# Third weight tile behind a norm, feed-forward banks and the place of two ScalarE steps in a two-tower transformer kernel

## The chip, the cores and the metric
The kernel runs on one core of one Trainium2 chip. The metric is the device time of one execution in microseconds (us).

## The reference, cut to what matters
Two transformer blocks of model width 1024 follow each other on 512 latent tokens; 256 context tokens stand beside them. The first block has two layers, the second one layer with attention and one with a gating unit.

```python
for l in range(2):                                   # first block
    zx = modulate(rms_norm(x, norm1_g[l]), mx[0], mx[1]) @ w_in[l]      # and zc from ctx
    y_f = fourier_mix(zf, w_f)                       # DFT over positions and channels
    u = conv31(a * sigmoid(g)) + b_dw                # depthwise, 31 taps
    y_c = silu(layer_norm(u, ln_g, ln_b)) @ w_pw2    # the convolution's norm
    attn = latent attention, 8 heads of 64 + 32
    x = x + mx[2] * (concat([y_f, attn, y_c]) @ w_o[l])
    x = x + mx[5] * (square(relu(modulate(rms_norm(x)) @ w_mlp1)) @ w_mlp2)   # hidden 4096
x = rms_norm(x, final_norm_g)
for l in range(2):                                   # second block
    h = modulate(rms_norm(x), sh1, sc1)
    y = attention_mixer(h, ctx) if l == 0 else sgu_mixer(h)
    x = x + g1 * y
    z = conv3(modulate(rms_norm(x), sh2, sc2) @ w_up) + conv_b     # 2 * 2816 channels
    x = x + g2 * ((silu(z_gate) * z_up) @ w_down)
return rms_norm(x, final_norm)
```

`mx`, `sh`, `sc` and `g` are vectors made from the Silu of the conditions `c` by large weights (the modulation).

## The kernel before, in words
Activations lie transposed in SBUF: 128 channels on the partitions, tokens along the free dimension, eight chunks `k` of 128 channels. `CTX` is the 256 context tokens, `LAT` the 512 latent ones, `ALL` both.

Every product with a large weight is made in three terms, to get near fp32 from the faster fp32r format: each value is split in a high part and a low part, and a tile sums high x high, low activations x high weights, and high activations x low weights. The weights come as 346 tiles of 128 x 1024 through `w_raw` (four buffers). For tile `n` ScalarE copies the high part into `w_hi` (`split`, L758), and GpSimd subtracts for the low part into `w_lo` (`w_low`, L672). Both have two buffers, so tile `n` may be split only when TensorE is done with tile `n - 2`. `ahead(n)` on ScalarE is `split(n + 2)`; it stands at the head of tile `n`'s work there. TensorE waits for `lo_ready` before a tile, then runs 8 chunks x 3 terms = 24 matmuls for each of the column ranges.

Behind a norm the first two tiles are run together and in two column parts (`parted_pair`, L1524; `first_tokens`, L1559, for the token-major tiles of the gating unit), as the normed chunks come in one by one. The third tile behind a norm is then an ordinary one: L1406 (`tile`) in the input projections, L1812 (`quarter`) in the first block's feed-forward, L2004 (`turn` in `ffn`) in the second block's, L1424 (`token_major`) in the gating unit. It needs the first tile's weight buffer back, and the first tile's PSUM bank.

A tile's result goes to `bank(2 * (t % 2) + b)`; `b` is 0 for context and 1 for latent columns. Latent tiles thus alternate between banks 1 and 3. `drained[t % 2]` counts the tiles read out of them. In the second block's feed-forward (`ffn`) a turn of the loop has four tiles (gate, up, gate, up): ScalarE applies the middle tap (L1317), VectorE the two outer taps out of PSUM (L2753, L2758), ScalarE the Silu (L1324), VectorE the product (L2765), ScalarE its high part (L1328), VectorE its low part (L2768). In the first feed-forward of the second block, VectorE also makes modulation products (L2270) between them; in the first block's it makes them beside L2571, which empties the hidden tiles' banks.

The order on each engine is written out by hand. On ScalarE in the input projections of a layer: split, (second layer only: Silu of the conditions, L914), copy of the first tile out of PSUM (L879), next split, (first layer only: that Silu), square.

The latent attention loops over units of 256 queries (`d`). In iteration `d` TensorE runs scores of unit `d + 1` (L1671), pv of unit `d - 1` (L1732), the transposes of unit `d` (`turn`, L1718), and then the sums of the convolution's norm (`pe_ln`, L1747 and L1753) in a few late iterations. ScalarE runs `ev(d - 1)` (the copies of the transposed probabilities, L999, for which pv waits), projections' copies, `exps(d + 1)` (L988), `pv_hi(d - 1)` (L1010), and last `act_ln`, the norm's squares (L1018) or its root (L768, L770). The squares wait for VectorE (L2455), which waits for TensorE's first sum. VectorE's low part of pv's result is L2445; pv waits for it too.

Of the kernel before, what the change touches and what calls it, by code (L numbers as in the profile page):

```python
# [17 lines left out]

# [94 lines left out]
def two_towers(nc, a):  # L113
    ctx = ExitStack()
    with ctx:
# [633 lines left out]
        def _(act):  # L749
# [146 lines left out]
            for layer in (0, 1):  # L896
# [154 lines left out]
                for d in range(n_units + 1):  # L1051
                    if d:
                        ev(d - 1)
                    if d - 1 in behind:
                        proj_ev(behind[d - 1])
# [8 lines left out]
                    for x in ln_stages(layer, d):  # L1064
                        act_ln(*x)
# [234 lines left out]
            def ffn(layer, tb, shifts):  # L1300
                nf = N_FFN[layer]
                pair0 = 0
                for part, kk in enumerate(FFN_PARTS):
# [4 lines left out]
                    with act.Fori(0, kk // 2) as i:  # L1308
                        for j in range(4):
# [7 lines left out]
                            nc.scalar.activation(dst, bank(2 * (t % 2) + 1), ACT.Identity,  # L1317
# [77 lines left out]
        def _(pe):  # L1395
            def tile(n, j, t, cols, rhs_hi, rhs_lo, per_k=None, first=True):

                pe.wait_ge(lo_ready, n + 1)
                if first:
                    slot_free(t)  # L1400
                for k in range(8):
                    if per_k:
                        per_k(k)
                    for wt, x in ((whi3, rhs_hi), (whi3, rhs_lo), (wlo3, rhs_hi)):
                        for (s0, s1), b in both(cols):
                            mm = pe.matmul(bank(2 * (t % 2) + b, c1=s1 - s0), wt[:, j % 2, k, :],  # L1406
                                           x(k, s0, s1), start=(k == 0 and wt is whi3 and x is rhs_hi),
                                           stop=(k == 7 and wt is wlo3))
                mm.then_inc(tile_done, 1)

            def token_major(n, toks, b0, off, ready=None):

                for h in range(2):
                    pe.wait_ge(lo_ready, n + h + 1)
                    w_hi, w_lo = (x[:, (n + h) % 2].rearrange("p k m -> p (k m)")
                                  .rearrange("p (k m) -> p k m", k=4) for x in (whi3, wlo3))
                    for k in range(4):
                        kk = 4 * h + k
                        if ready:
                            ready(kk)  # L1420
                        for tok in range(toks):
                            xs = slice(off + tok * P, off + (tok + 1) * P)
                            for q, (x, wt) in enumerate(((hi3, w_hi), (lo3, w_hi), (hi3, w_lo))):
                                mm = pe.matmul(bank(b0 + tok // 2, c0=256 * (tok % 2),  # L1424
# [1654 lines left out]
```

## Time and profile before

| what | value |
|---|---|
| median of 3 runs | 2860.78 us (2856.76 to 2861.16) |
| the profiled execution's own time | 2860.61 us |
| its span in the profile | 2858.8 us |
| mean granted clock of TensorE | 0.995 |
| TensorE busy | 2755.0 us (96%) |
| ScalarE, VectorE, GpSimd busy | 1121.6, 1624.5, 1142.0 us |
| transfers | 303.89 MB, 106 GB/s on average |

The profile's rows are of one execution. PE is TensorE (PEld its weight loads), DVE VectorE, ACT ScalarE, POOL GpSimd; L1406 is line 1406 of the kernel. Times of rows are microseconds from the span's start. A busy TensorE is one with a matmul in flight; the clock that was granted to it is given as a share of 2.4 GHz.

### The profile page before, as it was taken

To read this page: it belongs to the slowest core of one execution; us is meant where nothing else is said; L and a number is where in the kernel's file an instruction comes from. 1 tells how busy PE (TensorE), PEld (TensorE's weight loads), DVE (VectorE), ACT (ScalarE), POOL (GpSimd) and SP (SyncE) were. 2 spreads that over 40 slices of the span, in tenths; PEclk is the share of its full clock that TensorE was granted. 3 is DMA by queue.
4 is the path that set the end of the run, shared out by engine and by line. 5 is a ranking of instruction groups with operands and counts; after the bars stand their busy time and mean duration, and the time that the engine had idled before them with its cause. 6 is when DMAs were issued, how large, how long until landed. Compare 5 with 4: busy or idle time off the path is not lost.

```text
span 2858.8 us, 39710 instructions
## 1 busy us (share of the span) xinstructions
PE 2755.0 (96%) x14728; PEld 2224.8 (78%) x14728; DVE 1624.5 (57%) x2354; ACT 1121.6 (39%) x1850; POOL 1142.0 (40%) x554
## 2 busy tenths in 40 slices
PE   6999899999999999999999999889999999999998
PEld 4755588888888766688888788668888889888887
DVE  4877576555646577478455654766634642533133
ACT  4345533121212436542233523664433444443242
POOL 1399333323232368144444331004444443444443
PEclk9999999999999999999999999999999999999999
DMA  7500043332333320035454211003544532222222
GB/s 288 211 1 1 1 148 112 110 129 107 123 112 118 114 108 1 23 114 200 165 191 155 74 67 38 1 9 104 185 161 141 189 118 89 79 98 96 96 96 81
DMA packets 83498, 303.89 MB, mean 106 GB/s; under 512 B 9120, under 2 KB 12704, under 8 KB 82464
## 3 DMA queue, kind: packets, MB, share of 16 engines
q1 hardware_dynamic: 83072, 298.43, 29.4%
q10 hardware_dynamic: 288, 3.55, 0.3%
q8 instruction: 96, 1.57, 0.2%
q14 instruction: 42, 0.34, 0.0%
HBM read 299.84 MB, written 2.10 MB: 106 GB/s over the span
## 4 chain that ended last, share of the span: by engine, by line
PE 56%; DVE 4%; ACT 2%; issue 2%; POOL 0%; DVEq 0%; ACTq 0%; POOLq 0%
PE psum L2004 16%; PE psum L1812 11%; PE psum L1406 9%; PE psum L2025 8%; PE psum L1424 2%; PE psum L1495 2%; PE psum L1879 1%; PE psum L1671 1%; DVE psum L2165 1%; PE psum L1900 1%; DVE tiny L2674 1%; DVE in_lo L2155 1%; PE psum L1690 0%; PE psum L1917 0%; PE psum L1732 0%
## 5 line engine op out<-in xcount | busy, mean ns | idle before, releaser
L672 POOL TENSOR_TENSOR w_lo<-w_raw,w_hi 128x1024 fp32r<-128x1024 f32 x346 | 865.3, 2501 | 1633.0 <-ACT w_hi L758 1632.9
L758 ACT ACTIVATE w_hi<-w_raw 128x1024 fp32r<-128x1024 f32 x346 | 366.9, 1060 | 1244.7 <-PE psum L1812 556.1
L2251 DVE SCALAR_TENSOR_TENSOR residual<-psum,modulation,residual 128x512 f32<-128x512 f32 (+1 forms) x150 | 99.6, 684 | 342.6 <-PE psum L1812 145.9
L2270 DVE CUSTOM_DVE_ANT_0 mod_w<-mod_w,conditions 128x1024 f32<-128x1024 f32 x176 | 288.4, 1648 | 3.3
L2004 PE MATMUL psum<-in_hi,w_hi 128*128 128x512 f32 x672 | 262.3, 390 | 3.8 <-POOL w_lo L672 3.8
L2004 PE MATMUL psum<-in_lo,w_hi 128*128 128x512 f32 x672 | 262.1, 390 | 0.0
L2004 PE MATMUL psum<-in_hi,w_lo 128*128 128x512 f32 x672 | 262.0, 390 | 0.0
L1812 PE MATMUL psum<-in_hi,w_hi 128*128 128x256 f32 (+1 forms) x720 | 218.6, 358 | 2.2 <-POOL w_lo L672 2.2
L1812 PE MATMUL psum<-in_hi,w_lo 128*128 128x256 f32 (+1 forms) x720 | 219.0, 359 | 0.0
L1812 PE MATMUL psum<-hidden_hi,w_hi 128*128 128x256 f32 (+1 forms) x720 | 218.3, 358 | 0.5 <-DVE hidden_lo L2537 0.2
L1812 PE MATMUL psum<-hidden_hi,w_lo 128*128 128x256 f32 (+1 forms) x720 | 218.4, 358 | 0.0
L1812 PE MATMUL psum<-in_lo,w_hi 128*128 128x256 f32 (+1 forms) x720 | 215.9, 355 | 0.0
L1812 PE MATMUL psum<-hidden_lo,w_hi 128*128 128x256 f32 (+1 forms) x720 | 215.5, 354 | 0.0
L1406 PE MATMUL psum<-in_hi,w_hi 128*128 128x256 f32 (+1 forms) x576 | 191.6, 376 | 3.3 <-ACT mixer_space L879 1.9
L1406 PE MATMUL psum<-in_hi,w_lo 128*128 128x256 f32 (+1 forms) x576 | 184.4, 363 | 0.0
L1406 PE MATMUL psum<-in_lo,w_hi 128*128 128x256 f32 (+1 forms) x576 | 183.3, 361 | 0.0
L2753 DVE SCALAR_TENSOR_TENSOR small_w<-psum,vectors,small_w 128x511 f32<-128x511 f32 x88 | 65.9, 749 | 186.3 <-ACT small_w L1317 186.2
L2571 DVE TENSOR_TENSOR scratch<-psum,scratch 128x256 f32<-128x256 f32 (+1 forms) x96 | 54.8, 598 | 187.5 <-ACT scratch L1097 187.5
L1812 PEld LDWEIGHTS psum<-in_hi,w_hi 128*128 128x128 f32 x720 | 135.8, 189 | 24.5 <-POOL w_lo L672 2.8
L1812 PEld LDWEIGHTS psum<-hidden_hi,w_hi 128*128 128x128 f32 x720 | 135.5, 188 | 24.1 <-DVE hidden_lo L2537 2.5
L1812 PEld LDWEIGHTS psum<-in_lo,w_hi 128*128 128x128 f32 x720 | 136.1, 189 | 20.8
L1812 PEld LDWEIGHTS psum<-hidden_lo,w_hi 128*128 128x128 f32 x720 | 135.7, 189 | 20.4
(322 smaller groups left out, 5935.8 us busy)
## 6 DMA issues: line engine op xcount, KB each, us to landing
w_raw<-stream_dram SPq DMA_DIRECT2D x346, 512.0 KB, 4.1
mod_w<-mods_dram SPq DMA_DIRECT2D x176, 512.0 KB, 3.5
mixer_space<-first_mods_dram SPq DMA_DIRECT2D x12, 512.0 KB, 14.8
small_w<-small_w_dram SPq DMA_DIRECT2D x2, 2048.0 KB, 13.5
in_hi_space<-dft_x_dram SPq DMA_DIRECT2D x2, 2048.0 KB, 8.9
residual<-tokens_dram ACTq DMA_DIRECT2D x1, 3072.0 KB, 10.6
in_lo_space<-first_mods_dram SPq DMA_DIRECT2D x4, 512.0 KB, 16.2
conditions<-conditions_dram SPq DMA_DIRECT2D x2, 1024.0 KB, 11.7
```

The lines of the kernel that those rows point to most:

```text
L672: nc.gpsimd.tensor_tensor(wlo[:, (j % 2) * 1024:(j % 2 + 1) * 1024], raw3[:, j, :], whi[:, (j % 2) * 1024:(j % 2 + 1) * 1024].bitcast(F32) ...
L758: nc.scalar.activation(whi[:, (j % 2) * 1024:(j % 2 + 1) * 1024], raw3[:, j, :], ACT.Copy).then_inc(hi_ready, 1)
L1406: mm = pe.matmul(bank(2 * (t % 2) + b, c1=s1 - s0), wt[:, j % 2, k, :], x(k, s0, s1), start=(k == 0 and wt is whi3 and x is rhs_hi), stop= ...
L1424: mm = pe.matmul(bank(b0 + tok // 2, c0=256 * (tok % 2), c1=256 * (tok % 2) + 256), x[:, kk, xs], wt[:, k, :], start=(kk == 0 and q == 0 a ...
L1495: mm = pe.matmul(part_out(t + i, cols, p), wt, x, start=(k, q) == terms[0], stop=(k, q) == terms[-1])
L1812: mm = pe.matmul(bank(2 * (t % 2) + b, c1=s1 - s0), wt[:, n % 2, k, :], x[:, k, s0:s1], start=(k == 0 and q == 0), stop=(k == 7 and q == 2))
L2004: mm = pe.matmul(bank(2 * (t % 2) + 1), wt[:, n % 2, k, :], x[:, k, NC_:T], start=(k == 0 and q == 0), stop=(k == 7 and q == 2))
L2025: mm = pe.matmul(bank(2 * (t % 2) + 1), wt[:, n % 2, block_no % 8, :], x[:, k, :], start=(k == 0 and q == 0), stop=(k == kk - 1 and q == 2))
L2251: last = nc.vector.scalar_tensor_tensor(res3[:, m, s0:s1], bank(2 * (t % 2) + b, c1=s1 - s0), M(block_, chunk, m, 1 - b), res3[:, m, s0:s1 ...
L2270: nc.vector.tensor_tensor_reduce(w_tile, w_tile, cvec[:, 0:D], 1.0, 0.0, ALU.mult, ALU.add, dots[:, q:q + 1]).then_inc(mod_done, 1)
L2571: last = nc.vector.tensor_tensor(x, bank(2 * (t % 2) + b, c1=s1 - s0), x, ALU.mult)
L2753: side = nc.vector.scalar_tensor_tensor(x[:, 1:NX], bank(2 * (t % 2) + 1, c1=NX - 1), vec[:, bass.ds(i * 4 + col, 1)], x[:, 1:NX], ALU.mul ...
```

## The change
It has four parts.
1. The third tile behind a norm (`third`) waits only for its high part, runs its 16 matmuls with high weights first, then waits for the low part and runs the other 8. It applies in both input projections, the first quarter of both feed-forwards of the first block, the first turn of both feed-forwards of the second, and the first half of the gating unit's second token-major pair.
2. The four tiles of a turn in `ffn` go to four banks (1, 3, 0, 2; `turn_out`). The third and fourth tiles of a turn wait for one drained tile less.
3. In the second layer of the first block the Silu of the conditions stands behind the next split, as in the first layer.
4. On ScalarE `act_ln` moves from the end of iteration `d` to behind `ev(d)` in the next iteration.

```diff
+        def turn_out(t, j):
+            return bank(2 * ((t + j) % 2) + 1 - j // 2)
...
-                if layer:
-                    condition_silu()
                 copy_out(t0, lambda x, y: ckv[:, 0, x:y], ALL)
                 at_step(1)
-                if not layer:
-                    condition_silu()
+                condition_silu()
...
                 for d in range(n_units + 1):
                     if d:
                         ev(d - 1)
+                        for x in ln_stages(layer, d - 1):
+                            act_ln(*x)
...
                         pv_hi(d - 1)
-                    for x in ln_stages(layer, d):
-                        act_ln(*x)
...
-            def tile(n, j, t, cols, rhs_hi, rhs_lo, per_k=None, first=True):
-                pe.wait_ge(lo_ready, n + 1)
+            def tile(n, j, t, cols, rhs_hi, rhs_lo, per_k=None, first=True, third=False):
+                pe.wait_ge(hi_ready if third else lo_ready, n + 1)
                 if first:
                     slot_free(t)
-                for k in range(8):
-                    if per_k:
+                for k, q in terms(third):
+                    if per_k and q == 0:
                         per_k(k)
...
+                    if third and (k, q) == (0, 2):
+                        pe.wait_ge(lo_ready, n + 1)
...
+            def terms(third):
+                return sorted([(k, q) for k in range(8) for q in range(3)],
+                              key=lambda x: third and x[1] == 2)
...
-                    tile(n0 + j, (n0 + j) % 4, t0 + j, cols, in_hi, in_lo)
+                    tile(n0 + j, (n0 + j) % 4, t0 + j, cols, in_hi, in_lo, third=j == 2)
...
+                            third = first and j == 2
-                            pe.wait_ge(lo_ready, i * 4 + (n + 1))
-                            pe.wait_ge(drained[t % 2], i * 2 + t // 2)
+                            pe.wait_ge(hi_ready if third else lo_ready, i * 4 + (n + 1))
+                            pe.wait_ge(drained[t % 2], i * 2 + t // 2 - j // 2)
...
-                                    mm = pe.matmul(bank(2 * (t % 2) + 1), wt[:, n % 2, k, :],
+                                mm = pe.matmul(turn_out(tb_part, j), wt[:, n % 2, k, :],
...
-                token_major(N_SGU + 2 * c, 4, 2 * (t % 2), NC_)
+                token_major(N_SGU + 2 * c, 4, 2 * (t % 2), NC_, third=c == 1)
```

`quarter` and `token_major` are changed as `tile` is; ScalarE and VectorE read the turns' banks by `turn_out` too.

## Rows read from the trace of the kernel before

**Rows 1.** The page's busy times, with shares of the span and instructions.
```profile
PE 2755.0 (96%) x14728; PEld 2224.8 (78%) x14728; DVE 1624.5 (57%) x2354; ACT 1121.6 (39%) x1850; POOL 1142.0 (40%) x554
```
**Rows 2.** TensorE's waits: line, who ended them, total us, times, longest us.
```profile
PE psum L2004 <- POOL w_lo L672: 3.8, 2, 1.9
...
PE psum L1732 <- ACT in_hi_space L999: 3.5, 2, 2.8
...
PE psum L1812 <- POOL w_lo L672: 2.2, 2, 1.9
...
PE psum L1406 <- POOL w_lo L672: 0.6, 2, 0.4
```
**Rows 3.** Timeline of TensorE: start, duration, instruction, in brackets the idle time before.
```profile
989.39 0.47 PE L1406 MATMUL psum<-in_hi,w_hi 128*128 128x512 f32 x1 [1.89 <-ACT mixer_space L879]
...
1254.22 0.50 PE L1812 MATMUL psum<-in_hi,w_hi 128*128 128x512 f32 x1 [1.87 <-POOL w_lo L672]
...
1981.22 0.47 PE L2004 MATMUL psum<-in_hi,w_hi 128*128 128x512 f32 x1 [1.93 <-POOL w_lo L672]
...
2349.45 0.35 PE L1424 MATMUL psum<-w_hi,in_hi 128*128 128x256 f32 x1 [1.26 <-POOL w_lo L672]
...
2496.53 0.64 PE L1524 MATMUL psum<-in_hi,w_lo 128*128 128x256 f32 x4
...
2499.08 0.47 PE L2004 MATMUL psum<-in_hi,w_hi 128*128 128x512 f32 x1 [1.92 <-POOL w_lo L672]
```
**Rows 4.** Windows: us, TensorE busy (matmuls), granted clock, DMA share, GB/s.
```profile
316.00:320.00 4.00, 4.00 (x33) 0.57 0.02 4
336.00:341.00 5.00, 4.55 (x38) 0.66 0.00 0
1254.00:1259.00 5.00, 4.78 (x14) 0.66 0.00 0
...
2499.00:2504.00 5.00, 4.92 (x22) 1.00 0.60 202
```
**Rows 5.** Timeline of ScalarE, second layer's input projections.
```profile
984.20 1.06 ACT L758 ACTIVATE w_hi<-w_raw 128x1024 fp32r<-128x1024 f32 x1 [3.64 <-PE psum L1524]
...
986.57 1.91 ACT L914 ACTIVATE conditions<-conditions 128x2048 f32<-128x2048 f32 x1
```
**Rows 6.** Timelines of VectorE and ScalarE, second layer's first feed-forward tiles.
```profile
1252.26 0.69 DVE L2571 TENSOR_TENSOR scratch<-psum,scratch 128x512 f32<-128x512 f32 x1 [3.05 <-ACT scratch L1097]
...
1258.49 0.68 DVE L2571 TENSOR_TENSOR scratch<-psum,scratch 128x512 f32<-128x512 f32 x1
...
1261.63 1.06 ACT L758 ACTIVATE w_hi<-w_raw 128x1024 fp32r<-128x1024 f32 x1 [1.79 <-PE psum L1812]
```
**Rows 7.** Timelines of VectorE, ScalarE and GpSimd, second block's first feed-forward turn.
```profile
1982.13 3.38 DVE L2270 CUSTOM_DVE_ANT_0 mod_w<-mod_w,conditions 128x1024 f32<-128x1024 f32 x1
...
1988.59 1.06 ACT L758 ACTIVATE w_hi<-w_raw 128x1024 fp32r<-128x1024 f32 x1
...
1989.73 2.40 POOL L672 TENSOR_TENSOR w_lo<-w_raw,w_hi 128x1024 fp32r<-128x1024 f32 x1 [5.30 <-ACT w_hi L758]
...
1992.02 1.22 DVE L2270 CUSTOM_DVE_ANT_0 mod_w<-mod_w,conditions 128x1024 f32<-128x1024 f32 x1
...
1994.03 1.06 ACT L758 ACTIVATE w_hi<-w_raw 128x1024 fp32r<-128x1024 f32 x1 [3.72 <-PE psum L2004]
```
**Rows 8.** Timelines of VectorE, TensorE and ScalarE around the first layer's convolution norm.
```profile
313.94 0.58 DVE L2445 TENSOR_TENSOR in_lo<-psum,in_hi 64x128 fp32r<-64x128 f32 x2
...
315.98 2.67 PE L1732 MATMUL psum<-in_lo_space,mixer_space 128*64 128x128 f32 x24 [2.31 <-ACT in_lo_space L999]
...
322.14 2.74 PE L1671 MATMUL psum<-mixer_space 96*128 96x512 f32 x8
...
334.90 0.47 ACT L768 ACTIVATE mixer_space<-psum,tiny 128x256 f32<-128x256 f32 x1
...
336.45 2.66 PE L1732 MATMUL psum<-in_hi_space,mixer_space 128*64 128x128 f32 x24 [2.85 <-ACT in_hi_space L999]
```

More of the change, by code:

```diff
@@ L19 @@
+import itertools
 from contextlib import ExitStack
@@ L1403, in tile @@
                         per_k(k)
[L1404 to L1408, printed above, removed]
+                    if third and (k, q) == (0, 2):
+                        pe.wait_ge(lo_ready, n + 1)
@@ L1409, in tile @@
+                    wt, x = ((whi3, rhs_hi), (whi3, rhs_lo), (wlo3, rhs_hi))[q]
+                    for (s0, s1), b in both(cols):
+                        mm = pe.matmul(bank(2 * (t % 2) + b, c1=s1 - s0), wt[:, j % 2, k, :],
+                                       x(k, s0, s1), start=(k, q) == (0, 0), stop=(k, q) == (7, 2))
                 mm.then_inc(tile_done, 1)
-            def token_major(n, toks, b0, off, ready=None):
+            def terms(third):
+                return sorted([(k, q) for k in range(8) for q in range(3)],
+                              key=lambda x: third and x[1] == 2)
@@ L1413, in token_major @@
+            def token_major(n, toks, b0, off, third=False):
                 for h in range(2):
-                    pe.wait_ge(lo_ready, n + h + 1)
+                    late_lows = third and h == 0
+                    pe.wait_ge(hi_ready if late_lows else lo_ready, n + h + 1)
                     w_hi, w_lo = (x[:, (n + h) % 2].rearrange("p k m -> p (k m)")
                                   .rearrange("p (k m) -> p k m", k=4) for x in (whi3, wlo3))
-                    for k in range(4):
+                    order = sorted(itertools.product(range(4), range(toks), range(3)),
+                                   key=lambda x: late_lows and x[2] == 2)
+                    for k, tok, q in order:
@@ L1418, in token_major @@
                         kk = 4 * h + k
[L1419 to L1424, printed above, removed]
-                                                    c1=256 * (tok % 2) + 256),
-                                               x[:, kk, xs], wt[:, k, :],
-                                               start=(kk == 0 and q == 0 and tok % 2 == 0),
-                                               stop=(kk == 7 and q == 2 and tok % 2 == 1))
+                        if late_lows and (k, tok, q) == (0, 0, 2):
+                            pe.wait_ge(lo_ready, n + 1)
@@ L1429, in token_major @@
+                        xs = slice(off + tok * P, off + (tok + 1) * P)
+                        x, wt = ((hi3, w_hi), (lo3, w_hi), (hi3, w_lo))[q]
+                        mm = pe.matmul(bank(b0 + tok // 2, c0=256 * (tok % 2), c1=256 * (tok % 2) + 256),
+                                       x[:, kk, xs], wt[:, k, :],
+                                       start=(kk == 0 and q == 0 and tok % 2 == 0),
+                                       stop=(kk == 7 and q == 2 and tok % 2 == 1))
                     mm.then_inc(tile_done, 1)
@@ L1803, in quarter @@
                         n, t = n1 + j, t1 + j
[L1804 removed]
+                        third = first and j == 2
+                        pe.wait_ge(hi_ready if third else lo_ready, i * MLP_STEPS + (n + 1))
                         pe.wait_ge(drained[t % 2], i * 8 + t // 2)
                         hi_, lo_ = (hi3, lo3) if j < 8 else (hid_hi3, hid_lo3)
[L1807 to L1808 removed]
+                        for k, q in terms(third):
+                            if j == 8 and q == 0:
                                 pe.wait_ge(hid_ready, i * 8 + (e0 + k + 1))
[L1810 to L1814 removed]
+                            if third and (k, q) == (0, 2):
+                                pe.wait_ge(lo_ready, n + 1)
+                            wt, x = ((whi3, hi_), (whi3, lo_), (wlo3, hi_))[q]
+                            for (s0, s1), b in both(cols):
+                                mm = pe.matmul(bank(2 * (t % 2) + b, c1=s1 - s0), wt[:, n % 2, k, :],
+                                               x[:, k, s0:s1], start=(k, q) == (0, 0), stop=(k, q) == (7, 2))
                         mm.then_inc(tile_done, 1)
```

24 lines of the change are left out of this document (9 added, 15 removed).

## The prediction, made before the change was run
> **What bounds the kernel.** I read the page's busy times first: TensorE is busy 2755.0 us of 2858.8 [rows 1], so the most that any reordering can give is the 104 us in which it is not, plus what it loses at a lower clock. Then the list of TensorE's waits: the reader is to see how little of it this change can reach. The ones that it names are TensorE waiting for the low part of a weight tile (POOL w_lo): 3.8 us in two waits at L2004, 2.2 us in two at L1812 (the longest 1.9, so the other 0.3), 0.6 us in two at L1406 (0.4 is a third tile of the first layer) [rows 2]. Then TensorE's timeline around each such wait, for what stands before and behind it [rows 3]; the granted clock by windows, since a wait may cost more than itself [rows 4]; and the timelines of ScalarE, VectorE and GpSimd at each place, to find what is late next [rows 5 to 8].
>
> **Two unit prices.** In the feed-forward, 22 matmuls of 512 columns start in 5 us at a granted clock of 1.00 (2.4 GHz) (the last row of [rows 4]), so one starts every 0.227 us and a tile of 24 takes 5.45 us. Matmuls of 256 columns follow each other every (0.64 - 0.28) / 3 = 0.12 us  (from the four matmuls at 2496.53, [rows 3]).
> The clock: behind the 1.87 us wait at 1254, and alike behind the 1.93 us one at 1981, five microseconds hold only 14 matmuls at a mean clock of 0.66, which is 1.2 GHz for most of the stretch; behind the 1.92 us wait at 2499 the clock stays at 1.00 [rows 3, 4]. 22 - 14 = 8 matmuls, less one for idle time at the window's start: 7 x 0.23 = 1.6 us, and I use 1.7. So a wait of some 1.9 us costs either 1.9 or 3.6 us, and the traces show no way to say which.
>
> **Third tiles, place by place.** A pair of tiles ends, ScalarE makes the high part of the third (1.06 us), GpSimd its low part (2.4 us), and TensorE waits for the low part though its first 16 matmuls could do without. After the change these 16 run first, 16 x 0.227 = 3.6 us, longer than the 2.4 us, so the low part itself is hidden everywhere; if GpSimd took over 3.6 us the rest would show. I credit the idle time plus the 0.12 to 0.16 us by which the last matmul's tail would have been overlapped.
> 1. Input projections, first layer: 0.37 + 0.16 = 0.5. Mixer feed-forward, first layer: 0.3 + 0.16 = 0.5. In both, 24 matmuls on 256 and 24 on 512 columns (8.3 us) hide all that follows [rows 2].
> 2. Input projections, second layer: the third tile waits not for weights but for ScalarE's copy out of the first tile's bank: 1.89 us, because the Silu of the conditions (1.91 us behind a 1.28 us table load) stands ahead of it [rows 3, 5]. With the Silu behind the next split, the copy comes right behind the third tile's split, which ends at 985.3 [rows 5], and TensorE goes on at 987.35: 2.0. Cover for the moved Silu: it ends near 991.8, and what queues behind it is the square for the key norm and the split of the fifth tile. The split may start only when the third tile is done (987.35 + 5.45 = 992.8), and TensorE asks for the square a tile later still. In the first layer the Silu stays where it was: 0.
> 3. Mixer feed-forward, second layer (1254): the pair ends at 1252.2, but the third tile writes the first tile's bank, which VectorE's product (L2571) empties only at 1252.26 + 0.69 = 1253.0 [rows 6]. It then runs to 1258.45. What is late next: the fourth tile's bank. VectorE is held in a long modulation product (L2270, like the 3.38 us one of [rows 7], where the next takes 1.22), and its L2571 for the second tile ends at 1258.49 + 0.68 = 1259.2 [rows 6]. Today ScalarE sees the third tile done at 1261.63 and the fourth starts about 0.2 before that, 1261.4. So 1261.4 - 1259.2 = 2.2, of which 1.7 is the clock that does not fall after waits of 0.8 and 0.7 instead of 1.87. If it falls all the same: 0.5.
> 4. Second block's first feed-forward (1981): four banks are what lets the third tile start at 1979.3, as bank 0 has been empty since the norm; with two, it would wait for VectorE's second product. It ends at 1984.7, the fourth at 1990.2. What is late next is the fifth tile: VectorE's 3.38 us modulation product holds up the hidden product, that holds up ScalarE, whose split of the fifth tile starts at 1988.59, and GpSimd's low part is ready at 1989.73 + 2.40 = 1992.1 [rows 7]. None of these starts depends on the third tile. Today the fifth tile starts about 1993.8 (ScalarE sees the fourth done at 1994.03). Gain 1993.8 - 1992.1 = 1.7; a new wait of 2.0 us stands ahead of the fifth tile, and if the clock falls behind it, 0. I take 0.9, the middle, since two of the three feed-forward waits of this length cost the clock and one did not.
>    The row shows the modulation product at 3.38 us while GpSimd subtracts, 1.22 without [rows 7]. The Trainium skill (SBUF — State Buffer, "SBUF: two separate sides") calls the port pair that VectorE and GpSimd share an exclusive lock: the loser blocks for the other's whole instruction. By that rule the block comes back after the change; were it a mere coincidence of this run, the fifth tile would not be late and this place would give 3.4.
> 5. Token-major tiles of the gating unit (2349): 1.26 + 0.16 = 1.4; its 32 early matmuls last 32 x 0.12 = 3.8 us [rows 3].
> 6. Second feed-forward (2499): 1.92 + 0.12 = 2.0. VectorE has no modulation products here, so nothing is late next [rows 3].
> In the rest of the feed-forward turns TensorE never waits for a bank, so four banks there give 0. The reordered matmuls and weight loads are as many as before: 0 in both directions, bounded by the 0.16 us of one start.
>
> **Convolution norm.** First layer: TensorE first waits for the GpSimd taps, untouched. Then pv waits 2.31 us at 315.98 for ScalarE's copies, which stand behind the norm's squares [rows 8]. With the copies first, pv waits for VectorE's low part, 313.94 + 0.58 = 314.5: 1.4. Behind 315.98 the clock is 0.57 over 4 us [rows 4]; pv (24 matmuls, 2.67 us there, 1.53 at full clock), the turn and the norm's sum end at 322.14. At full clock they take 4.7 instead of 6.2: 1.4 more if the clock holds. At 336.45 pv waits 2.85 us again, with the clock at 0.66 behind it [rows 4, 8], now for copies behind the root (Ln and Exp, 334.90 to about 335.8): 0.9, and 1.1 to 1.5 for the clock behind it. Sum 1.4 + 1.4 + 0.9 + 1.5 = 5.2 if the clock holds throughout, 2.3 if it falls as before; below nothing only if squares or root came too late for TensorE's next sum, and they are ready over 1 us ahead. I take 4.4, nearer the upper end, as the waits shrink to about 1.0 and 1.8 us.
> Second layer: the squares stand ahead of copies too, worth 3.5 - 2.8 = 0.7 at first [rows 2], but the next exponentials follow VectorE's low part and minimum, which do not move: 0.
>
> **Sum.** 0.5 + 0.5 + 2.0 + 2.2 + 0.9 + 1.4 + 2.0 + 4.4 = 13.9, and I round to 14. From the profiled execution's 2860.61 (its span is 2858.8, the median 2860.78, so it is a typical run): 2846.5 us. The forecast's own range, 2843 to 2851, is the sum with clocks holding everywhere (17) to clocks falling at half of the places (10).
>
> **Rivals.**
> - *The waits only move.* The clock falls behind the new waits at 1258, 1990 and in both norm places: 0.5 + 0.5 + 2.0 + 0.5 + 0 + 1.4 + 2.0 + 2.3 = 9.2, 2851.4. For it: the clock fell at four of the five waits of 1.87 to 2.85 us named here for weights or copies (not at 2499); against: two of the four new waits are under 1 us. Chance 0.20.
> - *ScalarE's norm order is worth nothing,* because VectorE's low part bounds pv as it does in the second layer: 14 - 4.4 = 9.6, 2851.0. Against it stands the 2.85 us wait, in which VectorE's part has been done. Chance 0.12.
> - *The change doesn't reach the end.* The saved time is eaten by the next transfer or chain that runs on its own clock, as GpSimd's taps might in both layers. That would leave the places after the attentions: under 5, 2856 to 2860. Against it: no TensorE wait on a weight transfer exists in the list, and the taps start when TensorE's tiles end. Chance 0.06.
> - *Slower: the four banks upset the clock.* If the turns, moving through four banks, brought one fall per turn, 22 turns x 1.7 = 37 us less 14: 2884. From 9 falls on it decides. Against it: the mixer's 256+512-column tiles use four banks today at full clock. Chance 0.05. The Trainium skill (TensorE: Matmul & The Clock Gate, "A second HAM failure mode: psum-queue depth-cycling") tells of a kernel whose cycling through PSUM banks made the clock swing between its two levels; no run here shows it.
> - The forecast: 0.57.
>
> **Numbers.** Faster than 0.2% (5.7 us, below 2855.1; about what this kernel's three runs, 4.4 us apart, can tell): the forecast, the first two rivals less their upper tails, 0.85. Within: 0.10. Slower: 0.05. Range 2839 to 2855: the low end takes the clock holding everywhere and better luck elsewhere (the three runs differ by 4.4), the high end both middle rivals with 4 us of spread.
>
> **What would show it.** Right: no POOL w_lo wait at the third tiles; L2004's first wait becomes one of about 2 us on the fifth tile around 1981; 989's wait gone; pv's two ScalarE waits at 316 and 336 replaced by shorter VectorE ones; clock at 1.00 around 1255. Wrong: a fall of the clock at a place that has none today, a drained-bank wait at 1253 much beyond 0.8, or a wait at 2502 or 2508, which I hold to be free.

## The result and the profile after

| | time |
|---|---|
| predicted | 2846.5 us (2839 to 2855) |
| after, median of 20 runs | 2847.84 us (2845.67 to 2852.36) |
| before, median of 20 runs beside them | 2854.88 us (2848.90 to 2862.55) |
| ratio, 95% interval | 0.9977 (0.9969 to 0.9985) |
| span of the profiled execution, before and after | 2858.8 and 2844.8 us |

The change makes the kernel faster by 7.0 us in the medians, by 14.0 us in the two profiled executions. Both numbers are true, and the distance between them is what the experiments had to explain.

The page after, its busy times (against [rows 1]: TensorE 4.3 us less busy, so 9.7 of the 14.0 us were idle time):
```profile
PE 2750.7 (97%) x14728; PEld 2222.1 (78%) x14728; DVE 1632.9 (57%) x2354; ACT 1121.6 (39%) x1850; POOL 1149.6 (40%) x554
```
TensorE's waits after (line, who ended them, total us, times, longest):
```profile
PE psum L1742 <- DVE in_lo L2459: 5.6, 10, 2.0
...
PE psum L2019 <- DVE small_w L2772: 2.9, 2, 1.9
...
PE psum L1825 <- DVE scratch L2585: 1.3, 2, 0.8
...
PE psum L1825 <- DVE hidden_lo L2551: 0.9, 2, 0.7
```
The weights' low part has gone from the third tiles (only 0.2 us of it is left, at L1410, in the second block's input projections, as before), and so has ScalarE's name from the pv waits [rows 2]. VectorE stands in both places. (Lines moved: 2004 is 2019 now, 1812 is 1825, 1406 is 1410, 1732 is 1742, 1424 is 1435; on VectorE 2270 is 2284, 2445 is 2459, 2571 is 2585, 2758 is 2772.)

Timeline of TensorE after, at the places of [rows 3] and [rows 8]:
```profile
313.64 1.53 PE L1742 MATMUL psum<-in_lo_space,mixer_space 128*64 128x128 f32 x24 [0.23 <-DVE in_lo L2459]
...
331.69 1.54 PE L1742 MATMUL psum<-in_hi_space,mixer_space 128*64 128x128 f32 x24 [2.04 <-DVE in_lo L2459]
...
979.89 0.39 PE L1410 MATMUL psum<-in_hi,w_hi 128*128 128x512 f32 x1
...
1243.64 0.47 PE L1825 MATMUL psum<-in_hi,w_hi 128*128 128x512 f32 x1 [0.75 <-DVE scratch L2585]
...
1249.90 0.47 PE L1825 MATMUL psum<-in_hi,w_hi 128*128 128x512 f32 x1 [0.56 <-DVE scratch L2585]
...
1282.84 0.50 PE L1825 MATMUL psum<-hidden_hi,w_hi 128*128 128x512 f32 x1 [0.69 <-DVE hidden_lo L2551]
...
1982.09 0.49 PE L2019 MATMUL psum<-in_hi,w_hi 128*128 128x512 f32 x1 [1.87 <-DVE small_w L2772]
...
1988.82 0.47 PE L2019 MATMUL psum<-in_hi,w_hi 128*128 128x512 f32 x1 [1.00 <-DVE small_w L2772]
...
2485.12 0.40 PE L2019 MATMUL psum<-in_hi,w_hi 128*128 128x512 f32 x1
```
Windows of it (us, TensorE busy, granted clock, DMA share, GB/s), to be held against [rows 4]: at these places the clock stays at 1.00 where it had fallen.
```profile
316.00:320.00 4.00, 4.00 (x17) 1.00 0.02 4
331.00:336.00 5.00, 4.09 (x56) 1.00 0.02 5
1243.00:1248.00 5.00, 4.36 (x19) 1.00 0.00 0
1982.00:1987.00 5.00, 4.91 (x22) 1.00 0.51 143
```

Where the 14.0 us of the profiled pair lie, from the starts of the same matmuls in both timelines, and what the prediction gave:

| place | forecast | profiled pair |
|---|---|---|
| all up to GpSimd's taps at 309 (third tile of layer 0 among it) | 0.5 | -0.7 |
| convolution norm, layer 0 | 4.4 | 7.6 |
| feed-forward, layer 0 | 0.5 | 0.6 |
| conditions' Silu, layer 1 | 2.0 | 2.0 |
| attention of layer 1 | 0 | 0 |
| feed-forward, layer 1 (1254) | 2.2 | 0.7 |
| second block, first feed-forward (1981) | 0.9 | 0.3 |
| gating unit (2349) | 1.4 | 1.5 |
| second feed-forward (2499) | 2.0 | 2.1 |
| elsewhere | 0 | 0 |

The 7.6 us are not the edit's alone, as the section on the forecast shows.

### The profile page after: what moved, and what is told of

Its sections match the earlier page's. It is cut to its first block, busy times and chain, and to the rows that moved or that the text cites. A ratio compares the mean times of both kernels' runs of the same rounds, so it can differ in the third digit from the quotient of the medians.

```text
span 2844.8 us, 39710 instructions
## 1 busy us (share of the span) xinstructions
PE 2750.7 (97%) x14728; PEld 2222.1 (78%) x14728; DVE 1632.9 (57%) x2354; ACT 1121.6 (39%) x1850; POOL 1149.6 (40%) x554
## 4 chain that ended last, share of the span: by engine, by line
PE 83%; DVE 9%; ACT 4%; issue 3%; DMA 1%; SPq 1%; POOL 0%; DVEq 0%; ACTq 0%; POOLq 0%
PE psum L1825 28%; PE psum L2019 15%; PE psum L1410 13%; PE psum L2039 8%; PE psum L1435 2%; PE psum L1505 2%; PE psum L1681 2%; PE psum L1534 2%; PE psum L1891 1%; DVE tiny L2438 1%; PE psum L1700 1%; DVE psum L2179 1%; PE psum L1728 1%; PE psum L1742 1%; PE psum L1642 1%
## 5 line engine op out<-in xcount | busy, mean ns | idle before, releaser
L2284 DVE CUSTOM_DVE_ANT_0 mod_w<-mod_w,conditions 128x1024 f32<-128x1024 f32 x176 | 303.3, 1733 | 3.3
L1825 PE MATMUL psum<-in_hi,w_lo 128*128 128x256 f32 (+1 forms) x720 | 213.2, 354 | 0.0
L1410 PE MATMUL psum<-in_hi,w_hi 128*128 128x256 f32 (+1 forms) x576 | 190.5, 374 | 1.0 <-issue 0.7
L1410 PE MATMUL psum<-in_lo,w_hi 128*128 128x256 f32 (+1 forms) x576 | 183.3, 361 | 0.0
L1410 PE MATMUL psum<-in_hi,w_lo 128*128 128x256 f32 (+1 forms) x576 | 181.1, 361 | 0.0
```

What stands on the lines that cost most here:

```text
L1825: mm = pe.matmul(bank(2 * (t % 2) + b, c1=s1 - s0), wt[:, n % 2, k, :], x[:, k, s0:s1], start=(k, q) == (0, 0), stop=(k, q) == (7, 2))
L2284: nc.vector.tensor_tensor_reduce(w_tile, w_tile, cvec[:, 0:D], 1.0, 0.0, ALU.mult, ALU.add, dots[:, q:q + 1]).then_inc(mod_done, 1)
```

## The experiments

### The kernel before, three more profiles (e1, e5, e10)
No edit. What is asked is why the medians show half of what the profiles show.

> The kernel before, unchanged, for one more profile. The 20 runs of before fall in two groups, 2849 to 2853 and 2857 to 2863 us. Theory A (falls of the clock): a profile with a time in the low group shows the same waits of TensorE as the first one at the third tiles (1.9 us at the second layer's feed-forward and at both feed-forwards of the second block, 2.3 and 2.9 at the convolution norm), and its shorter time is clock that didn't fall behind them: up to 1.7 us at each of two third tiles and some 3 us at the norm. Theory B (loads): the groups differ in the first 40 us or in another wait for transfers, and the clock falls at the same places. If this profile is in the high group, its falls are where the first one's are (A) or anywhere (B).

> The kernel before once more, for a profile that may fall in its low group (2846 to 2853 us). In both profiles so far (high group) TensorE's clock falls behind the waits at 309, 316, 336, 1254 and 1981, each costing 1.6 to 1.7 us, 8.4 us together. Theory A (falls of the clock): a profile of the low group has the same waits and none or one of these falls. Theory C: it has other waits of TensorE than these two. If the profile is in the high group again, it must show at least four of the same falls.

> The kernel before, one more look. All three profiles of it so far are of the upper group (2860.3 to 2860.6 us). If this one is of the lower group (under 2853), its landmarks against the first profile show where the 10 us lie: by the theory of two courses in one stretch of the kernel, at a granted clock that is the same; by the rival spread over several places, 1.7 us each, with a fall of the clock missing at each.

e1: median 2849.09 us of 10 runs (2846.36 to 2861.55), ratio 0.9986 (0.9971 to 1.0002); e5: 2860.34, e10: 2850.27, one run each. Put together, the 124 runs of the kernel before that were made in this study fall in two groups with nothing between 2853.0 and 2855.4: 66 of them from 2846.2 to 2853.0 (median 2849.9) and 58 from 2855.4 to 2862.6 (median 2860.1). The first three profiles were all of the upper group. e5 already spoke against the clock: its text asked for four of the five falls of the first profile, and it has three (at 314, 334 and 1252) at the same time of 2860.3 us. e10's profile was of the lower group, and it shows where the 10 us lie. They are not at the waits, and not at a lower clock: 9.6 of the 10.3 us between its span and the first profile's are in the first layer's feed-forward (the other places differ by falls of the clock and by one wait, in both directions), a stretch in which TensorE never waits. Its windows in the first profile of the kernel before:
```profile
500.00:600.00 100.00, 100.00 (x568) 1.00 0.31 113
```
and in e10:
```profile
500.00:600.00 100.00, 100.00 (x579) 1.00 0.33 116
```
TensorE is 100% busy in both, the granted clock is 1.00 in both, and yet 100 us hold 568 matmuls in one and 579 in the other. (The second layer's feed-forward, with 512 columns alone, holds 441 in both.) From the first 0.95 us wait of the norm ahead of that feed-forward (426.98 in one, 424.48 in the other) to that of the norm behind it (976.15 and 964.09) pass 549.17 us or 539.61 us. A grouping of the matmuls between 500 and 900 by shape (total us, mean ns of one, idle) shows how; the kernel before, first profile:
```profile
L1812 PE MATMUL psum<-in_hi,w_lo 128*128 128x512 f32 x192 | 77.4, 403 | 0.0
L1812 PE MATMUL psum<-in_hi,w_hi 128*128 128x512 f32 x192 | 76.4, 398 | 0.0
L1812 PE MATMUL psum<-in_lo,w_hi 128*128 128x512 f32 x192 | 75.8, 395 | 0.0
```
and e10:
```profile
L1812 PE MATMUL psum<-in_hi,w_lo 128*128 128x512 f32 x192 | 75.1, 391 | 0.0
L1812 PE MATMUL psum<-in_hi,w_hi 128*128 128x512 f32 x192 | 75.1, 391 | 0.0
L1812 PE MATMUL psum<-in_lo,w_hi 128*128 128x512 f32 x192 | 75.1, 391 | 0.0
```
The stream of alternating 256 and 512 column matmuls has two courses: an even one, and one with a beat of three terms that is 1.9% slower. The even one was profiled in this feed-forward once, in e10; that a run of a lower group took it is inferred from its time. The choice falls at the first matmuls behind the 0.30 us wait of the third tile (that tile itself takes 8.58 us in the first profile and 8.44 in e10) and then holds for over 500 us. The slow course begins like this (kernel before; start, duration, here pairs of matmuls):
```profile
438.60 0.62 PE L1812 MATMUL psum<-in_hi,w_hi 128*128 128x256 f32 x2 [0.30 <-POOL w_lo L672]
439.05 0.51 PE L1812 MATMUL psum<-in_lo,w_hi 128*128 128x256 f32 x2
439.40 0.52 PE L1812 MATMUL psum<-in_hi,w_lo 128*128 128x256 f32 x2
439.76 0.52 PE L1812 MATMUL psum<-in_hi,w_hi 128*128 128x256 f32 x2
```
and the fast one like this (e10):
```profile
436.12 0.62 PE L1812 MATMUL psum<-in_hi,w_hi 128*128 128x256 f32 x2 [0.30 <-POOL w_lo L672]
436.57 0.51 PE L1812 MATMUL psum<-in_lo,w_hi 128*128 128x256 f32 x2
436.93 0.51 PE L1812 MATMUL psum<-in_hi,w_lo 128*128 128x256 f32 x2
437.27 0.51 PE L1812 MATMUL psum<-in_hi,w_hi 128*128 128x256 f32 x2
```
From the second row to the fourth pass 0.71 us in the first and 0.70 in the second, and over each tile behind the third 8.48 and 8.32.

### The edits alone (e2, e3, e4, e9)
e2 has parts 1 and 2 alone. e3 has part 4 alone, e9 parts 3 and 4. e4 is the whole change with two banks in the turns:
```diff
-            return bank(2 * ((t + j) % 2) + 1 - j // 2)
+            return bank(2 * ((t + j) % 2) + 1)
...
-                            pe.wait_ge(drained[t % 2], i * 2 + t // 2 - j // 2)
+                            pe.wait_ge(drained[t % 2], i * 2 + t // 2)
```

> The third tiles and the four banks alone; Silu and convolution norm as before. Theory A (the gains are separate and add): the waits on POOL w_lo at the third tiles are gone; saved by place, first block first layer 0.5 and 0.5 us, its second layer's feed-forward 0.7 to 2.2, the second block's first feed-forward 0.3 to 1.7, the gating unit 1.5, the second feed-forward 2.1; the 1.9 us wait for ScalarE's copy in the second layer's input projections stays. Sum 5.6 to 8.5 us by landmarks, 4 to 7 in the medians. Theory B (waits only move): within 0.2% of before.

> The convolution norm's place on ScalarE alone. Theory A (the copies behind squares and root are what pv waits for): the ScalarE waits of pv at 316 and 336 shrink, from the start of the taps' wait to the output projections 4 to 6 us less in the first layer, 0 to 0.7 in the second, 3 to 5 in the medians. Theory B (VectorE's low part bounds pv): under 1.5 us in the first layer. Either way the third tiles wait as before.

> The whole change, but with two banks in the second block's feed-forward as before. Theory A (the fourth tile needs four banks where VectorE makes modulation products): the third tile of the first feed-forward waits 0.3 to 2.0 us for the first tile's bank, and the fourth about 2.4 us, as VectorE empties the second tile's bank only 7.8 us after the pair ends; fifth and sixth then wait less than in the changed kernel, and the place ends within 1 us of it, before or after: the new waits there come from the modulation products, not the banks. In the second feed-forward, the third tile waits some 2 us for the bank, so 1.5 to 2 us of the gain is gone there. Theory B (banks do nothing): all places as in the changed kernel, within 0.3 us.

> The kernel before with parts 3 and 4 alone (ScalarE's convolution norm behind the next copies, the conditions' Silu behind the next split in the second layer); no third tiles, two banks. The times of the kernel before fall in two groups some 10 us apart (46 of 83 between 2846 and 2853 us, 37 between 2855 and 2863), those of the norm move alone in two groups too, those of every kernel with the third tiles in one. Theory: something in the kernel before takes one of two courses, and the third tiles or the banks hold it in the longer one, so that part of their gain is paid back. Then this kernel shows two groups again, the lower near 2850 - 2 - 5 = 2843, the upper near 2853, and its lower group is below every run of the whole change (2845.7 at the least). Rival: the two groups are a matter of the clock falling at more or fewer of the waits, which any of the four parts narrows; then this kernel has one group, near 2848 to 2851.

| kernel | runs | median, ratio to before (interval) | fast course | slow course |
|---|---|---|---|---|
| before | 124 | - | 66 runs, 2849.9 | 58 runs, 2860.1 |
| e3, norm order | 12 | 2854.35, 0.9995 (0.998 to 1.001) | 5 runs, 2845.3 | 7 runs, 2856.4 |
| e9, norm order and Silu | 12 | 2843.67, 0.997 (0.9955 to 0.9985) | 8 runs, 2843.1 | 4 runs, 2853.1 |
| e2, third tiles and banks | 12 | 2853.84, 1.0001 (0.999 to 1.0012) | none | 12 runs, 2853.8 |
| e4, two banks | 12 | 2849.36, 0.9984 (0.9973 to 0.9995) | none | 12 runs, 2849.4 |
| after | 20 | 2847.84, 0.9977 (0.9969 to 0.9985) | none | 20 runs, 2847.8 |

The runs of a row are sorted by their times: the gap is 5.5 us or more in e3 and e9, and there is none in e2, e4 and after, whose profiles all show the slow course. Column by column the parts add up: in the slow course the norm order is worth 3.7 us (fast course 4.6), the Silu 3.3 (2.2), the third tiles with the banks 6.2: 13.2 in sum, against 12.2 for the whole change. By medians over both courses the same edits seem to be worth nothing (e2, e3), because e2 loses the fast course and because e3 met it in 5 of 12 runs only, which may be chance. The courses of the runs are taken from their times.

The texts ahead of these runs fared so. e2: by starts of the same matmuls against the first profile of before it gains 0.5, 0.5, 0.7, -0.1, 1.5 and 2.2 us at its six places, 5.3 in sum where 5.6 to 8.5 were expected, and nothing of it in the median, where 4 to 7 were expected. The -0.1 is the second block's first feed-forward: the clock fell behind the fifth tile's new wait of 1.90 us. e3: 6.3 us from 309 to 399 against the first profile, 4.1 from 205 to 399 against e5, for 4 to 6 expected. e9: two groups where they were expected, 2843.1 and 2853.1, and the lower group (up to 2845.61) ends just under the lowest run of the whole change (2845.67). So the whole change, with a median of 2847.84, is not shown to be better than its parts 3 and 4 alone, with 2843.67: the intervals of their ratios overlap.

e4 shows what the four banks hold. Its third tile waits in both feed-forwards for VectorE's second outer tap (L2772; not for the product, as the prediction has it), which empties the first tile's bank:
```profile
PE psum L2019 <- DVE small_w L2772: 3.8, 2, 1.9
```
These are 1.93 us at 1971 and 1.92 us at 2487. With four banks the second is gone and the first has moved to the fifth tile. As expected, the first feed-forward ends 0.3 us behind that of the change, though the wait of about 2.4 us on the fourth tile did not come. The second one takes 3.7 us more than in the profile after, 1.9 of wait and the rest a fall of the clock behind it. The medians differ by 1.5 us and the intervals of the ratios overlap, so what the banks are worth over many runs stays open.

### VectorE's modulation products behind the second feed-forward's banks (e6, e7, e8)
After the change VectorE is what TensorE waits for at 1982 and 1988. Timeline of VectorE after, there:
```profile
1970.92 1.26 DVE L2284 CUSTOM_DVE_ANT_0 mod_w<-mod_w,conditions 128x1024 f32<-128x1024 f32 x1
...
1972.11 3.40 DVE L2284 CUSTOM_DVE_ANT_0 mod_w<-mod_w,conditions 128x1024 f32<-128x1024 f32 x1
...
1983.03 3.41 DVE L2284 CUSTOM_DVE_ANT_0 mod_w<-mod_w,conditions 128x1024 f32<-128x1024 f32 x1
```
and GpSimd's:
```profile
1968.67 5.76 POOL L677 TENSOR_TENSOR w_lo<-w_raw,w_hi 128x1024 fp32r<-128x1024 f32 x2 [3.25 <-ACT w_hi L763]
1979.59 5.76 POOL L677 TENSOR_TENSOR w_lo<-w_raw,w_hi 128x1024 fp32r<-128x1024 f32 x2 [5.16 <-ACT w_hi L763]
```
Each of GpSimd's rows holds two subtractions. The first lasts 2.4 us. The second starts at 1971.05, while the first product runs, and lasts 3.38 us, 1.0 more, to 1974.43; the second product, started at 1972.11, ends at 1975.51, 1.1 us behind that. With the product held, hidden product, ScalarE's split and GpSimd's low part are late; two splits then come close together (1978.47 and 1980.26), two subtractions back to back, and they hold the next turn's product in turn. That is read from the rows as the reason why there are two waits and not one; no run takes the hold away by itself. e6 moves the products of a turn behind the up tile's hidden low part; e7 leaves them and lets all four tiles of the first part's turns wait for one drained tile less; e8 has both, and in the second layer's first quarter starts the products one tile later.
```diff
-                            elif m0 is not None:
-                                for m in (j, j + 1):
+                            if is_up and m0 is not None:
+                                for m in (j - 1, j):
```
```diff
-                            pe.wait_ge(drained[t % 2], i * 2 + t // 2 - j // 2)
+                            pe.wait_ge(drained[t % 2], i * 2 + t // 2 - (j // 2 if first or part else 1))
```

> The whole change, with VectorE's modulation products in the second block's first feed-forward moved behind the hidden product of each pair of tiles, the same products in the same order. Theory A (the held modulation product makes fifth and sixth tile wait): the waits of 1.87 and 1.00 us for L2772 vanish, 2 to 3 us less by landmarks from the third tile to the end of that feed-forward, 1 to 3 in the median against the changed kernel. Theory B (ScalarE's or GpSimd's own order makes them late): the waits stay within 0.5 us.

> The whole change, with the first part's turns of the second block's feed-forwards waiting only for the tile that last used their own bank (one drained tile less for the first two tiles of a turn too). Theory A: the sixth tile's wait of 1.00 us vanishes, the fifth's 1.87 us stays within 0.2 us, because its weights' low part is ready at about the same time. So 1.0 us less by landmarks. Theory B (banks are what both wait for): both vanish, 2.9 us less.

> Both of these, and in the first quarter of the second layer's feed-forward the first tile's modulation products moved behind the seventh's place (made with the eighth's, beside the down tiles). Theory A (a modulation product held by GpSimd's subtraction makes the fourth tile wait, and VectorE runs behind for the eight hidden tiles): the 0.56 us wait at the fourth tile and the 0.69 us wait for the last hidden low part vanish, 1.3 to 2 us less there, and 3 us less in the second block's first feed-forward; in all 3 to 5 us under the changed kernel. Theory B (both come from ScalarE's order): no wait shrinks by more than 0.3 us there.

e6: 2872.41 us (6 runs, 2871.34 to 2873.19), ratio 1.0061 (1.0042 to 1.0081), 24.6 us slower than the whole change. Its waits of TensorE:
```profile
PE psum L2019 <- DVE small_w L2772: 17.0, 9, 2.5
...
PE psum L2039 <- DVE small_w L2772: 3.6, 2, 2.5
```
so 20.6 us in 11 waits where the change has 2.9 in two; three falls of the clock in the same stretch (2006, 2105, 2269) account for some 5 more, an estimate from 1.7 us each. One of the waits, 2.36 us at 2006.26, ends with VectorE's tap (L2772, 2005.46 to 2006.21). What VectorE did ahead of it, by its timeline in e6:
```profile
2001.24 3.41 DVE L2284 CUSTOM_DVE_ANT_0 mod_w<-mod_w,conditions 128x1024 f32<-128x1024 f32 x1
...
2004.58 0.74 DVE L2767 SCALAR_TENSOR_TENSOR small_w<-psum,vectors,small_w 128x511 f32<-128x511 f32 x1
```
A product that a subtraction holds now stands right ahead of the taps that empty a bank, turn after turn. e8: 2872.27 us (6 runs), ratio 1.0064 (1.0044 to 1.0084): the waits for VectorE's tap shrink from 20.6 to 12.2 us, and nine for the low part (5.9 us in total) come up instead; in the second layer the fourth tile's 0.56 us wait is gone, and the one for the hidden low part grows from 0.69 to 2.2 us. So the gains expected of e6 and e8 did not come. e7: 2847.47 us (12 runs, 2844.57 to 2849.76), ratio 0.9971 (0.9958 to 0.9983). As expected the wait of 1.00 us is gone and the one of 1.87 stays, as 1.90; but two of 0.53 and 0.24 us for the low part follow, and the feed-forward gains 0.2 us against before, where the change gains 0.3. The time can't be told from the change's. The old place of the products, between the gate tile's taps and the up tile's, is thus the better one. The sixth tile's wait was one for a count of drained tiles. The fifth tile's is not that alone: in e7 the low part of its weights is ready at 1985.06 and VectorE's tap ends at 1985.07, in the change at 1981.96 and 1981.97, so the profile's name for what ended it is a matter of 0.01 us.

### Which edit loses the fast course (e11, e12)
e11 is the whole change less the third tile of the first layer's feed-forward; e12 is the kernel before with that third tile alone.
```diff
-                        third = first and j == 2
+                        third = first and j == 2 and layer == 1
```

> The whole change less one third tile, that of the first layer's feed-forward, which runs in the old order behind its low part. In the profiles that feed-forward takes one of two courses: from the first waits of its norm to those of the next it lasts 549.2 us (three profiles of the kernel before, the norm move alone, norm and Silu) or 539.6 us (the fourth profile of the kernel before), each tile 8.48 or 8.32 us, at a granted clock of 1.00 and with no wait in either; all six profiles with the third tiles have the longer one, 548.6 us. Theory: the reordered third tile holds the stream of 256 and 512 column matmuls in the longer course. Then this kernel shows two groups of times, the upper at the whole change's 2848.4, the lower near 2838.5, with more than half of the runs in it (54 in 83 of the kernel before, 8 in 12 of norm and Silu), so a median of about 2840. Rival: another of the third tiles, or the banks, or the Silu decides; then one group at about 2848.4.

> The kernel before with one edit: the third tile of the first layer's feed-forward in the new order, behind its high part alone. Theory: it holds the feed-forward in the course of 548.6 us, so the lower group of the kernel before vanishes: all times between 2855 and 2862, a median near 2859.5 against about 2852 of the kernel before, so a change that saves a wait of 0.3 us makes the kernel 0.2 to 0.3% slower. Rival (another third tile decides): two groups as before, both 0.5 lower.

(The count for the kernel before in the first text is wrong: it was 46 of 83, as in the text of e9, or 54 of 100 with the 17 runs made beside e9.)

e12: median 2860.19 us, all 12 runs from 2858.78 to 2862.61, ratio 1.002 (1.0006 to 1.0035): slower, as expected. e11: 2846.55 us, three of 12 runs at 2835.24 to 2838.70 and nine from 2844.59 to 2849.96 (median 2847.3), ratio 0.9967 (0.9951 to 0.9983). Its profile is of the nine and shows the slow course. So one edit, on the smallest wait of all (0.3 us), takes the fast course away, alone as well as within the change: none of the 68 runs of e2, e4, e7, e12 and the whole change is in a lower group. By the times, its removal brings the course back. It came back in 3 of 12 runs and not in more than half as expected; whether that is chance is open. e12's matmuls between 500 and 900, grouped by shape, have the same beat of three, on other terms:
```profile
L1828 PE MATMUL psum<-in_lo,w_hi 128*128 128x512 f32 x192 | 77.4, 403 | 0.0
L1828 PE MATMUL psum<-in_hi,w_lo 128*128 128x512 f32 x192 | 76.4, 398 | 0.0
L1828 PE MATMUL psum<-in_hi,w_hi 128*128 128x512 f32 x192 | 75.8, 395 | 0.0
```
In the changed kernel the third tile starts without a wait, directly in the pair's stream, and its matmuls are 0.35 to 0.36 us apart from the start. Whether the missing pause or the new order of terms decides was not taken apart. By its ratio e11 (0.9967) is not told apart from e9 (0.997), which has no third tiles at all, nor from the whole change (0.9977). Its fast runs, 2837.3 us in the median, are the fastest of the study, 12.6 us below the fast runs of before; how often a run meets them decides what that is worth.

The two paces are not this feed-forward's alone, and the reordering does not always bring the slow one. The first layer's input projections alternate 256 and 512 columns too. From 84 to 112 us, at a granted clock of 1.00 and without a wait, the seven profiles without a reordered third tile there hold 160 or 161 matmuls, the seven with it 163 or 164; the first profile of before and the profile after:
```profile
84.00:112.00 28.00, 28.00 (x160) 1.00 0.54 197
...
84.00:112.00 28.00, 28.00 (x164) 1.00 0.62 218
```
Here the slow pace is the one without the reordering, and costs 0.7 us. Behind the attention (356 to 390 us) a tile takes 8.48 us in the first profile of before, in e6 and in e7, and 8.32 in the other eleven. e1 and e5 have 8.32 there and 8.48 in the feed-forward. So the pace is no state of the whole execution: each stream takes it anew.

## Why the forecast was right, and where it was not

The time came out 1.3 us above the forecast and inside its own range; the reason for it holds for one of the two courses. That the start was counted from a run of that course was luck.

**The step that failed** is the one that costs the order of the matmuls at nothing: "The reordered matmuls and weight loads are as many as before: 0 in both directions, bounded by the 0.16 us of one start." In the first layer's feed-forward the reordered tile takes away a course that saves 9.6 us and that, by their times, 66 of 124 runs of the kernel before have: over its runs, some 5 us given back (an estimate, 9.6 x 66 / 124) for a gain of 0.6. Beside it stands the sentence that the profiled execution "is a typical run". It and the three runs shown (2856.76 to 2861.16) were all of the upper group, that of the slow course. As the change has only that one, counting from a slow-course run gave the right time after, and twice the true difference: 14 against 7.0 in the medians, and against 12.2 between the slow courses.

**Third tiles.** As forecast, the weights' low part is hidden everywhere, and the input projections' Silu (2.0), the gating unit (1.5) and the second feed-forward (2.1) are within 0.1 us. The first layer's 0.5 of the input projections came, and 0.7 more by the pace, but they do not reach the end. Behind a wait of 2.65 us at 183 the clock fell in the profile after (granted 0.51 over the next 5 us, where the first profile of before has 1.00), and TensorE went from 0.7 us ahead to 4.1 behind at 190, yet was only 0.7 behind at 309: before, it waited there 3.2 us ahead of the norm's first sum, and that wait takes up what is lost ahead of it. e5 and e10, the kernel before with a fall at 184, have no such wait either. That is the mechanism of the rival "doesn't reach the end", at this place alone.

**1254: mis-sized, 0.7 for 2.2.** The two waits came as worked out (0.75 and 0.56 for 0.8 and 0.7) and the clock held; at 1249.90 the change was 2.1 us ahead. Then VectorE, at work without a pause and with its products held (three of 3.3 to 3.4 us where others take 1.23), emptied the banks late: the fifth and sixth tiles started 5.8 us behind the tile before, the seventh 5.5, instead of 5.44, which is 0.8 us; and in the ninth tile TensorE waited for the last hidden low part (0.69 at 1282.84). 1.4 us were gone by 1555. The prediction followed the chain for two tiles and should have done so for the quarter.

**1981: 0.3 for 0.9,** near the end where the clock falls, though it did not fall. The new wait on the fifth tile came (1.87 for 2.0), with VectorE's tap and the low part ready together, and at its start the change was 1.7 us ahead, as worked out for a clock that holds. What was missed is the sixth tile's 1.00 us: 1.3 of the 1.7 us were gone by its start. The Trainium skill (SBUF — State Buffer, "SBUF: two separate sides") has VectorE or GpSimd blocked for the other's whole instruction; the trace agrees, for both engines: the second subtraction, started while a product ran, lasts 3.38 instead of 2.40 us and ends at 1974.43, and the product started beside it lasts 3.40 instead of 1.22, so until 1.1 us behind that end.

**Convolution norm: 4.4 forecast.** In the profiled pair 7.6, with the clock at 1.00 behind both waits; between groups of the same course 3.7 and 4.6 us. The first profile of before has a fall behind its 3.2 us wait at 309, which no profile with the edit has, and 0.9 of the 7.6 us are the slow pace behind the attention. Against e5, which has neither, the change gains 5.6 us from 205 to 399, e3 with this edit alone 4.1. pv waits for VectorE's low part, 0.23 and 2.04 us for the forecast's "about 1.0 and 1.8". Profiles of the kernel before alone differ by 2.8 us up to 399, so the pair overstates the edit and the forecast has its size.

**The clock.** In the profile after no fall follows the new waits; in other profiles some do. Counted over all fourteen profiles, at half or full clock behind the same wait:

| TensorE's wait | us | profiles with it | with a fall behind it |
|---|---|---|---|
| norm, first, for ScalarE's copies (316) | 1.64 to 2.36 | 6 | 6 |
| norm, second, for the copies (336) | 2.85 | 6 | 6 |
| norm, second, after part 4 (332) | 2.04 | 8 | 4 (e3, e4, e6, e7) |
| second layer's input projections (989) | 1.89 | 7 | 3 (e2, e3, e12) |
| its feed-forward, third tile (1254) | 1.87 | 7 | 7 |
| the same after part 1 | 0.75 | 7 | 0 |
| second block, first feed-forward, third tile (1981) | 1.93 | 8 | 7 (not e5) |
| the same, fifth tile (1982 after) | 1.87 to 1.90 | 4 | 1 (e2) |
| second feed-forward, third tile (2499) | 1.92 | 8 | 6 (not before, e1) |

So the rival that the waits only move is wrong for the profile after and happens at single places in others, and its count was off: of the six waits of 1.87 to 2.85 us on weights or copies the clock fell behind four, not four of five, as the one at 989 had none. At 1981 and 2499 a fall costs 1.6 to 1.7 us; the longer one at 183 cost 4.8. Which waits of some 2 us bring one stays open. The forecast's own range was off as well: with every clock holding its terms add up to 15.5 us, not 17.

**Four banks** did not upset the clock: 1.00 through the turns, with 443 matmuls from 2050 to 2150 us for 442 before. The rival with nine or more falls found none in them. Something that slows the kernel was in the change all the same, by a mechanism that no rival named.

## What to carry to other kernels
Before a difference is sized from two profiles, look at how the times of the old kernel are spread: where they fall in two groups, find a profile of each and compare like with like. A reordering that saves a short wait can change the pace of the long stream behind it, so count matmuls per 100 us in the stretches without waits too. And where a wait is taken from an engine that had slack only because of it, follow the next engine for a whole loop and not for two tiles.

## What the runs showed of the hardware
TensorE's stream of alternating 256 and 512 column matmuls, never idle and at a granted clock of 1.00 throughout, ran at 568 or at 579 matmuls in 100 us in executions of the same kernel; the course was taken at the stream's start and kept for 500 us, and other streams of the same execution could have the other one. A stream of 512 columns alone (1350 to 1450 us) ran at 441 or 442 in all fourteen profiles. What makes the difference inside the engine is not shown by any row here.
